# Layer 1's attention: the second query's rotation moves to bank 2, the second values' transposes to bank 3

## The reference, cut to what matters

```python
q = (_rms_norm(h @ w_dq, q_norm) @ w_uq).reshape(bsz, s, 16, 64 + 32)
q_rope = _rotate(q[..., 64:], cos, sin)             # 32 of 96 features are rotated
kv = (c_kv @ w_ukv).reshape(bsz, s, 16, 64 + 64)    # c_kv: 256 latent features
k_nope, v = kv[..., :64], kv[..., 64:]
logits = (q_nope . k_nope + q_rope . k_rope) * 96 ** -0.5, causal
p = softmax(logits)
out = (p @ v) for 16 heads of 64, then @ w_o
```

## Time and profile before

| | |
|---|---|
| median of 3 runs | 3876.49 us (3874.75 to 3878.22) |
| profiled execution | 3876.09 us, span 3874.2 us |
| TensorE busy | 3639.7 us, 94% of the span |
| VectorE, ScalarE busy | 1871.2 us (48%), 1174.8 us (30%) |
| mean granted clock of TensorE | 0.974 |
| chain that ended last | PE 88%, DVE 7%, ACT 2% |
| layer 1's attention | from 950.7 to 1180.6 us |

### The profile page before, as it was taken

One profiled execution on the slowest core, in us unless ns is written; L12 is line 12 of the kernel. 1 busy time (PEld: TensorE's weight loads), 2 busy tenths in 40 slices (PEclk: granted clock), 3 DMA queues, 4 the chain that ended last, 5 costly groups with the idle time before them and its releaser, 6 DMA issues.

```text
span 3874.2 us, 48363 instructions
## 1 busy us (share of the span) xinstructions
PE 3639.7 (94%) x17514; PEld 2509.7 (65%) x17514; DVE 1871.2 (48%) x3826; ACT 1174.8 (30%) x2184; POOL 308.7 (8%) x355
## 2 busy tenths in 40 slices
PE   5999899998888999979999999999698999999989
PEld 2445488883444888846666666666355888888864
DVE  3744363635553635434454545444303666666641
ACT  1203210102333101023444444444201455555530
POOL 6700000000000000000000000000000222222200
PEclk8999899999999999999999999999798999999999
DMA  7521333422013334230101111111011222222211
GB/s 153 146 76 55 87 99 82 114 77 73 24 49 87 88 86 120 77 94 28 38 27 32 32 32 32 32 33 32 11 55 46 61 60 60 60 62 67 61 46 49
DMA packets 456581, 246.46 MB, mean 64 GB/s; under 512 B 44272, under 2 KB 448496, under 8 KB 456464
## 3 DMA queue, kind: packets, MB, share of 16 engines
q1 hardware_dynamic: 420528, 216.28, 20.3%
q0 software_dynamic: 14144, 28.36, 2.7%
q10 hardware_dynamic: 21792, 0.22, 0.4%
HBM read 229.96 MB, written 14.80 MB: 63 GB/s over the span
## 4 chain that ended last, share of the span: by engine, by line
PE 88%; DVE 7%; ACT 2%; issue 2%; ACTq 1%; DMA 0%; DVEq 0%; SPq 0%
PE bank L471 19%; PE bank L1743 13%; PE bank L333 10%; PE bank L2282 9%; PE bank L1729 5%; PE bank L1041 3%; PE bank L2301 3%; PE bank L1200 3%; PE bank L1111 2%; PE bank L1765 2%; PE bank L868 2%; PE bank L1090 2%; PE bank L1711 2%; PE bank L851 1%; PE bank L1753 1%
## 5 line engine op out<-in xcount | busy, mean ns | idle before, releaser
L1743 PE MATMUL bank<-hT,ring 128*128 128x512 f32 x1504 | 510.1, 491 | 1.0 <-ACT arena L1933 1.0
L1743 PEld LDWEIGHTS bank<-hT,ring 128*128 128x128 f32 x1504 | 278.4, 190 | 218.5 <-issue 204.6
L333 PE MATMUL bank<-big,ring 128*128 128x512 f32 (+1 forms) x1024 | 391.0, 545 | 5.3 <-ACTq L354 2.2
L333 PEld LDWEIGHTS bank<-big,ring 128*128 128x128 f32 x1024 | 196.4, 192 | 198.4 <-issue 185.1
L2332 POOL TENSOR_TENSOR tb<-ring 128x512 f32<-128x512 f32 x32 | 40.7, 1272 | 2946.9 <-DVE big L2800 2784.3
L1097 ACT ACTIVATE arena<-bank 128x512 f32<-128x512 f32 (+2 forms) x224 | 118.4, 529 | 430.0 <-PE bank L1090 429.1
L471 PE MATMUL bank<-big,arena 128*128 128x256 f32 x1024 | 228.8, 379 | 0.0
L471 PEld LDWEIGHTS bank<-big,arena 128*128 128x128 f32 x1024 | 194.6, 190 | 26.4
L1960 DVE TENSOR_REDUCE cols<-bank 128x1 f32<-128x768 f32 x128 | 116.5, 952 | 152.5 <-PE bank L1711 152.5
L1729 PEld LDWEIGHTS bank<-ring,hT 128*128 128x128 f32 x1536 | 175.2, 192 | 12.5 <-issue 12.5
L1729 PE MATMUL bank<-ring,hT 128*128 128x128 f32 x1536 | 178.3, 276 | 0.0
(11 more groups left out here) (338 smaller groups left out, 6077.7 us busy)
## 6 DMA issues: line engine op xcount, KB each, us to landing
ring<-in_mlp_w SPq DMA_DIRECT2D x128, 512.0 KB, 5.7
ring<-in_a_w_in SPq DMA_DIRECT2D x64, 512.0 KB, 4.0
ring<-in_b_w_in SPq DMA_DIRECT2D x64, 512.0 KB, 4.1
ring<-in_mod_w SPq DMA_DIRECT2D x48, 512.0 KB, 4.1
ring<-in_even_w_in SPq DMA_DIRECT2D x32, 512.0 KB, 4.0
bias_d<-tb POOLq DMA_DIRECT2D x96, 128.0 KB, 3.5
big<-bias_d POOLq DMA_DIRECT2D x16, 768.0 KB, 5.2
ring<-in_a_w_out SPq DMA_DIRECT2D x16, 512.0 KB, 4.0
```

Source lines behind the costliest of these rows:

```text
L333: mm = pe.matmul(bk(m % 2 + 2 * j)[:, 0:z - a], ring[s][:, k, :], ln.rhs(g * KT + k, a, z), start=g == 0 and k == 0, stop=g == ln.kg - 1 a ...
L1743: mm = pe.matmul(flatb[2][:, a:z], ring[s][:, k, :], hT[:, k, a:z], start=k == 0, stop=k == KT - 1)
```

## The change

The four users of bank 5 are spread over three banks. The first query's rotation and the first values' transposes stay in bank 5; the second query's rotation goes into bank 2, the second values' transposes into bank 3. On TensorE the first rotation comes at place 3 without the fourth projection, which moves to place 4; the second rotation moves from 4 to 5, the values' transposes from 5 and 6 to 6 and 7. VectorE's second rotation moves from place 5 to 6. ScalarE's second copy of keys and values moves from 4 to 5, and its two copies of transposed values go from 5 and 6 to place 7, one behind the other, ahead of that place's `act_turn`. The counter `vv` now counts VectorE's two reads of a rotation, `st` (which nobody waited for) ScalarE's two copies of transposed values. The second rotation waits for ScalarE's first copy of keys and values (`ga`), the first for the values' copies of the pair before (`st`). The first score product of a pair no longer waits for the transposed values; `att1.values` makes the first product with the values wait for them (`pe_pv` asks for it at its first tile). The first projection of a pair waits for the last pair's reads of the rotations, the second for its copies of transposed values.

```diff
@@ -1234,7 +1234,12 @@
             def f(pe, ph, g, e, u):
                 per = ph.rots
                 pe.wait_ge(ph.raw, g * per + (n + 1))
-                pe.wait_ge(ph.vv, g * ph.uses5 + ph.use5[("rot", n)])
+                if b == 5 and ph is att1:
+                    pe.wait_ge(ph.st, g * 2)
+                elif b == 5:
+                    pe.wait_ge(ph.vv, g * ph.uses5 + ph.use5[("rot", n)])
+                else:
+                    pe.wait_ge(ph.ga, g * 2 + 1)
                 pe.matmul(bk(b)[0:m, :], rot[0:m, 0:m], raw[0:m, :], start=True, stop=True).then_inc(ph.rot, 1)
             return f
 
@@ -1245,7 +1250,7 @@
         use5(att0, [("rot", 0), ("rot", 1)])
         att0.rots = 2
 
-        def rope_dve(n, raw, tmp, tab, b, j, write, m=P, shared=True):
+        def rope_dve(n, raw, tmp, tab, b, j, write, m=P, shared=True, turned=5):
 
             def evac(dve, ph, g, e, u):
                 multiplied(dve, ph.name, 4 * e + j, u)
@@ -1258,7 +1263,7 @@
             def fin(dve, ph, g, e, u):
                 dve.wait_ge(ph.rot, g * ph.rots + (n + 1))
                 dve.wait_ge(ph.gd, g * ph.rots + (n + 1))
-                dve.tensor_tensor(raw[0:m, :], bk(5)[0:m, :], tab[1][0:m, :], ALU.mult).then_inc(ph.vv, 1)
+                dve.tensor_tensor(raw[0:m, :], bk(turned)[0:m, :], tab[1][0:m, :], ALU.mult).then_inc(ph.vv, 1)
                 dve.wait_ge(ph.vv, g * ph.uses5 + (ph.use5[("rot", n)] + 1))
                 for dst, h in write(e):
                     mm = dve.tensor_tensor(dst, tmp[h, :], raw[h, :], ALU.add)
@@ -1413,26 +1418,31 @@
         v1 = lambda e, k: ar1(e, 2048 + P * k, P)
         att1 = Pairs("att1", 4, 8, 96 ** -0.5, lambda t: P * (t + 1), k1, q1, v1,
                      lambda e, s, t: cz[:, 512 - P * (t + 1):512], lambda t: list(range(t + 1)), out0)
-        use5(att1, [("rot", 0), ("rot", 1), "vA", "vB"])
+        use5(att1, [("rot", 0), ("rot", 1)])
         att1.rots = 2
         Q96 = slice(0, 96)
         qA_ev, qA_fin = rope_dve(0, rA, tA, cs1, 2, 0, lambda e: [(ar1(e, 0, 512)[Q96, :], Q96)], 96, False)
-        qB_ev, qB_fin = rope_dve(1, rB, tB, cs1, 3, 1, lambda e: [(ar1(e, 512, 512)[Q96, :], Q96)], 96, False)
+        qB_ev, qB_fin = rope_dve(1, rB, tB, cs1, 3, 1, lambda e: [(ar1(e, 512, 512)[Q96, :], Q96)], 96, False, 2)
 
         def kv_act(n, raw):
 
             def f(act, ph, g, e, u):
                 multiplied(act, ph.name, 4 * e + 2 + n, u)
-                act.activation(ar1(e, 1024 + 512 * n, 512)[LO, :], bk(2 + n)[LO, :], ACT.Copy).then_inc(ph.st, 1)
+                act.activation(ar1(e, 1024 + 512 * n, 512)[LO, :], bk(2 + n)[LO, :], ACT.Copy)
                 act.activation(raw, bk(2 + n), ACT.Copy).then_inc(ph.ga, 1)
             return f
+
+
+
+        VB = (5, 3)
 
         def v1_pe(n, raw):
             def f(pe, ph, g, e, u):
                 pe.wait_ge(ph.ga, g * 2 + (n + 1))
-                pe.wait_ge(ph.vv, g * 4 + (2 + n))
+                if n == 0:
+                    pe.wait_ge(ph.vv, g * 2 + 1)
                 for t in range(4):
-                    m = pe.transpose(bk(5)[:, P * t:P * t + P], raw[:, P * t:P * t + P], ident)
+                    m = pe.transpose(bk(VB[n])[:, P * t:P * t + P], raw[:, P * t:P * t + P], ident)
                 m.then_inc(ph.vt, 1)
             return f
 
@@ -1440,8 +1450,8 @@
             def f(act, ph, g, e, u):
                 act.wait_ge(ph.vt, g * 2 + (n + 1))
                 dst = ar1(e, 2048, 512).rearrange("p (t d) -> p t d", t=4)[:, :, 64 * n:64 * n + 64]
-                act.activation(dst, bk(5).rearrange("p (t d) -> p t d", t=4)[:, :, 64:128], ACT.Copy)\
-                    .then_inc(ph.vv, 1)
+                act.activation(dst, bk(VB[n]).rearrange("p (t d) -> p t d", t=4)[:, :, 64:128], ACT.Copy)\
+                    .then_inc(ph.st, 1)
             return f
 
         def qlat(k, a, z):
@@ -1449,19 +1459,21 @@
 
         def kvlat(k, a, z):
             return lat[:, 3 + k, a:z]
-        fA, fB = by_act(2, 0), by_act(2, 0)
+        fA = lambda pe, ph, g: pe.wait_ge(ph.vv, g * 2)
+        fB = lambda pe, ph, g: pe.wait_ge(ph.st, g * 2)
         att1.pe = [job(0, 2, 0, 3, 3, fA, m=96, rhs=qlat), job(1, 3, 0, 3, 3, fB, m=96, rhs=qlat),
-                   job(2, 2, 0, 2, 2, by_dve(2, 1), rhs=kvlat),
-                   both_(job(3, 3, 0, 2, 2, by_dve(2, 2), rhs=kvlat), rot_pe(rA, rotm, 0, m=96)),
-                   rot_pe(rB, rotm, 1, m=96), v1_pe(0, vA), v1_pe(1, vB), nothing]
-        att1.dve = [nothing, qA_ev, qB_ev, nothing, qA_fin, qB_fin, nothing, nothing]
-        att1.act = [nothing, nothing, nothing, kv_act(0, vA), kv_act(1, vB), v1_act(0), v1_act(1), nothing]
+                   job(2, 2, 0, 2, 2, by_dve(2, 1), rhs=kvlat), rot_pe(rA, rotm, 0, m=96),
+                   job(3, 3, 0, 2, 2, by_dve(2, 2), rhs=kvlat), rot_pe(rB, rotm, 1, b=2, m=96),
+                   v1_pe(0, vA), v1_pe(1, vB)]
+        att1.dve = [nothing, qA_ev, qB_ev, nothing, qA_fin, nothing, qB_fin, nothing]
+        att1.act = [nothing, nothing, nothing, kv_act(0, vA), nothing, kv_act(1, vB), nothing,
+                    both_(v1_act(0), v1_act(1))]
 
         def ready1(pe, p):
             pe.wait_ge(att1.prod, p * 2 + 2)
-            pe.wait_ge(att1.vv, p * 4 + 4)
             pe.wait_ge(att1.ga, p * 2 + 2)
         att1.ready = ready1
+        att1.values = lambda pe, p: pe.wait_ge(att1.st, p * 2 + 2)
 
         uq = d["odd_w_uq"][0].rearrange("(k p) n -> p k n", p=P)
         ukv = d["odd_w_ukv"][0].rearrange("(k p) n -> p k n", p=P)
```

## The result

The changed kernel takes 3845.85 us (median of 4 runs, 3841.58 to 3849.16), the kernel before 3875.62: a ratio of 0.9922, 95% interval 0.9905 to 0.9939. It is faster by 0.8%, inside the range of 3833 to 3853 and 6 us above the predicted 3840. On a second chip the same kernel had 3843.04 against 3875.1, 0.9924 (0.9905 to 0.9943).

A forecast was written before the change was run, and what follows sets the result against it. TensorE, busy 94% of the span, was taken as the bound, losing time in layer 1's attention to waits and a lowered clock. 3876.1 - 21.8 - 3.0 - 11.4 = 3839.9, said as 3840; range 3833 to 3853, forecast's own 3834 to 3845.

The forecast's parts named there:

- Waits removed and the transposes moved: Layer 1's attention: three waits and tails go, first values' transposes move behind the last score product: 3.13 + 0.58 = 3.71 us a pair.
- the third score product is fed: Earlier part of a pair: the maximum it needs is just ready; up to 0.1 us a pair may be lost.
- What is late next: Behind the last score product: VectorE's second rotation, moved to place 6, delays the seventh head-tile's transposes by 0.6 us.
- Per pair: Each of seven pairs produced beside another's attention: 3.71 - 0.6 = 3.1 us won, 21.8 together.
- The first pair: The pair produced alone: rotation starts earlier and only VectorE's rotation precedes the first score product; 3.0 us won.
- The clock inside the pairs: Falls go with the waits: three pairs give back 8.9 us, the first pair about 2.5; 11.4 together.
- Rivals A: Layer 1's attention: the clock falls stay, in three or four pairs; 3851 us, chance 0.15.
- rival B: Behind the last score product: the new weak stretch makes the clock fall in every pair; 3861 us, chance 0.05.
- the step that took the last pair as a witness: New order's weakest stretch keeps the clock, since the last pair, TensorE busy 13.08 of 20 us, lay at 1.00.
- the sign "the granted clock at 1.00 from the first pair's score products to the stage's end": Profile after, layer 1's attention: clock expected at 1.00 throughout; stretches still at 0.50 would prove the clock forecast wrong.
- 2 to 4 us for where other stages' short falls lie: Other stages: allowance in the forecast's own range for short clock falls shifting once all behind comes earlier.
- rival C: VectorE becomes the bound: second rotation's whole 1.41 us on the path, 0.1 more at third score product; 3846, chance 0.07.

The follow-up runs named there:

- the trace with the waits filled: Kernel before, with one spare product (result unused) added in each of its two 1.2 us waits per pair: 3870.63 us against 3874.71, 0.9988.
- the places-alone run: Changed kernel with its new order of steps, but all four uses back in bank 5, each waiting for the one before: 3881.72 us, 1.0012.
- the last pair's waits filled: Changed kernel meant to get nine spare products in the last pair's waits; by an edit error only the last was in: 3839.08 us.

## Why the prediction was right, and where it was off

- *Waits removed and the transposes moved:* 3.71 us up to the last score product was predicted, 20.28 - 16.49 = 3.79 came. The waits are gone, and the third score product is fed: it follows the product with the values by 0.38 (1014.34 to 1014.72).
- *What is late next:* 0.6 was predicted behind the last score product. It is 6.23 in the pair shown (1019.82 to 1026.05) where it was 5.63: 0.6. But in four of the six pairs after the first it is 6.02 or 6.03: 0.4. With VectorE's move undone it is 5.46, so the move costs 0.56 in those four and about 0.8 in the other two, near the 0.6 taken; for that difference among the pairs the trace names no cause. What the prediction had a little wrong is the start of the product with the values, taken as unchanged at 4.33 behind the last score product: it is 4.16 (1019.82 to 1023.98). The wait is the one named, L1090 for L1082. Without the move a pair is 0.7 shorter, so the price was right and there was no need to pay it: the product is done in time for place 5. The prediction costed the move and did not ask that.
- *Per pair* 3.1 was predicted; from 179.94 at full clock to 157.04 it is 22.9 / 7 = 3.3. The first pair gave 3.2 to 3.9 for 3.0; the two traces of the change differ in it by the same projections at another clock (16 matmuls listed at 9.43 and 10.09).
- *The clock inside the pairs:* 11.4 was predicted; the trace with the waits filled is 11.15 below that of before. Rivals A and B are out for the seven pairs, which were at 1.00 in every trace of the change.
- *The two rules of the Trainium skill* (TensorE: Matmul & The Clock Gate). By the one on idle gaps ("Why this matters for your kernels"), taken alone, the falls would not hang on these waits; the trace with the filled waits speaks against that, at 1.3 us or less each. By the one on transposes (Part 4: PE-mode transpose) rival B should have come; the new stretch of five groups of transposes stayed at 1.00 in every trace of the change. In the places-alone run, where waits of 1.19 and 1.68 stand between transposes, it fell in each pair; which of the two did it, the transposes or the length of the waits, no run separates.
- *What failed* is the step that took the last pair as a witness ("attended alone, has TensorE busy for 13.08 of 20 us, also at 1.00"). One trace at 1.00 didn't prove that the stretch is safe: it fell in the first trace after, for 8.3 us there and a part of the 7.5 behind. So the sign "the granted clock at 1.00 from the first pair's score products to the stage's end" did not come in that trace. And "2 to 4 us for where other stages' short falls lie" was too small: the changed kernel's ten runs reach from 3829 to 3852. The sum holds up to the last pair, where 38 us came for 36.2. That falls elsewhere make 3845.85 of 3840 is argued from the two traces: in the first the stretches outside the sum add 10.2 us (15.8 lost in the last pair and behind it, 5.6 won ahead of the stage), in the second they take 9.2 off.
- *Where luck helped.* 3845.85 lies just outside the forecast's own range (3834 to 3845) and at rival C's 3846; only the rows tell the two apart, for C asks 0.9 more a pair and the pairs are at 22.6. And with 10.2 us more in one execution and 9.2 less in another, that the median came within 6 of 3840 is in part the chance of which falls came; two of the ten runs, at 3829, lie below the range.

## What to carry to other kernels

When several short uses share one accumulator bank, the waits between them can cost twice, as idle time and, as here, once more as clock: read the granted clock in the microseconds behind the waits before pricing them. Give each use a bank of its own where one is free for that moment, then order the steps so that what each needs is done a place earlier, and check for each engine that a step moved later was not ready earlier. Where a wait can't go, products of a later step can be moved into it: ten of the next projection cost 1.2 us here and saved 8.6.

## What the hardware showed that was not expected

Useless products in the waits made the seven pairs 11 us faster in the trace. And the clock of the same instructions falls in different stretches from one execution to the next: ahead of the stage, where no instruction differs, the stretch from 360 to 405 (in layer 0) was at 0.66 in three of the ten traces (before, the places alone, the last pair's waits filled) and at 0.92 in the other seven. The trace of before and the second one of the changed kernel reach the stage 7.7 us apart (950.72 and 943.00):

```profile
360.00:405.00 45.00, 34.31 (x187) 21.17 (x186) 19.10 (x76) 13.93 (x38) 0.00 (x0) 0.66 0.09 24
```

```profile
360.00:405.00 45.00, 34.15 (x202) 20.04 (x202) 18.81 (x76) 15.04 (x40) 0.00 (x0) 0.92 0.13 36
```

A difference of a few us between two kernels can therefore be read here from the stage's own rows, and not from the whole time.
